# Output products on one TensorE: who makes the low parts, where the conditioning steps and the norm weights stand

## The reference

```python
# conditioning of each layer: six vectors, one per 1024 columns
m = silu(c) @ w_ada + b_ada                      # shift, scale, gate (attention); shift, scale, gate (feed-forward)
# layer 0
new = x + g_a * (concat(oa, ob) @ w_out)         # the output product
h = rmsnorm(new) * (1 + sc_f) + sh_f
new = new + g_f * ((silu(h @ w_gate) * (h @ w_up)) @ w_ffn_out)
# layers 1 and 2
x = layer_norm(ALPHA * x + m[2] * (att @ w_out), ln_g, ln_b)
f = conv_ffn(x * (1 + m[4]) + m[3], w_up, conv_w, conv_b, w_down)
x = layer_norm(ALPHA * x + m[5] * f, ln_g, ln_b)
```

## Time and profile before

| | us |
|---|---|
| median of 3 runs | 2566.37 (2564.48 to 2567.72) |
| profiled execution | 2561.57 |
| its span, first to last instruction | 2559.8 |
| TensorE matmul busy | 2373.7 (93%) |
| VectorE busy | 1601.5 (63%) |
| ScalarE busy | 969.5 (38%) |
| POOL busy | 361.4 (14%) |
| mean granted TensorE clock | 0.971 of full |

### The profile page before, as it was taken

One profiled execution on the slowest core, in us unless ns is written; L12 is line 12 of the kernel. 1 busy time (PEld: TensorE's weight loads), 2 busy tenths in 40 slices (PEclk: granted clock), 3 DMA queues, 4 the chain that ended last, 5 costly groups with the idle time before them and its releaser, 6 DMA issues.

```text
span 2559.8 us, 33225 instructions
## 1 busy us (share of the span) xinstructions
PE 2373.7 (93%) x13210; PEld 1916.1 (75%) x13210; DVE 1601.5 (63%) x2696; ACT 969.5 (38%) x1792; POOL 361.4 (14%) x355
## 2 busy tenths in 40 slices
PE   6987998999998899898989999999988998999996
PEld 3865566888887778566778888888877776788875
DVE  3538676565656742676768775556454986765455
ACT  4325453322212512567242232322432773424232
POOL 0110102100012200000400213223121000101133
PEclk9999999999999999999999999999999998999998
DMA  6221014744534312111322342333112103332321
GB/s 242 93 95 58 25 58 173 250 157 140 181 106 149 108 50 76 50 48 43 140 71 82 99 140 79 112 115 132 46 70 74 34 30 117 134 115 83 107 91 50
DMA packets 79163, 257.59 MB, mean 101 GB/s; under 512 B 5665, under 2 KB 10401, under 8 KB 70561
## 3 DMA queue, kind: packets, MB, share of 16 engines
q1 hardware_dynamic: 65024, 205.01, 23.3%
q0 software_dynamic: 12688, 46.14, 5.2%
q10 hardware_dynamic: 1296, 4.30, 0.4%
HBM read 246.00 MB, written 9.44 MB: 100 GB/s over the span
## 4 chain that ended last, share of the span: by engine, by line
PE 60%; DVE 13%; issue 10%; ACT 7%; POOL 3%; DMA 2%; POOLq 0%; ACTq 0%; DVEq 0%
PE PS L1036 8%; PE PS L1037 8%; PE PS L1038 8%; PE PS L1107 5%; PE PS L1108 4%; PE PS L1109 4%; PE PS L897 3%; PE PS L800 3%; PE PS L797 3%; PE PS L798 3%; PE PS L910 2%; ACT HT L2354 2%; PE PS L941 2%; DVE SM L1752 2%; PE PS L840 1%
## 5 line engine op out<-in xcount | busy, mean ns | idle before, releaser
L1036 PE MATMUL PS<-HH,WH 128*128 128x512 f32 (+1 forms) x1088 | 424.4, 390 | 13.9 <-DVE WL L1926 6.0
L1037 PE MATMUL PS<-HL,WH 128*128 128x512 f32 (+1 forms) x1088 | 420.7, 387 | 0.0
L1038 PE MATMUL PS<-HH,WL 128*128 128x512 f32 (+1 forms) x1088 | 420.4, 386 | 0.0
L2217 ACT ACTIVATE WH<-STG 128x1024 fp32r<-128x1024 f32 (+1 forms) x204 | 198.9, 1022 | 300.0 <-PE PS L1109 237.3
L1926 DVE TENSOR_TENSOR WL<-STG,WH 128x1024 fp32r<-128x1024 f32 (+1 forms) x204 | 239.0, 1212 | 47.1 <-ACT WH L2217 47.1
L1107 PE MATMUL PS<-WH,AH 128*128 128x512 f32 x616 | 244.5, 397 | 14.1 <-DVE WL L1926 5.0
L1036 PEld LDWEIGHTS PS<-HH,WH 128*128 128x128 f32 x1088 | 207.2, 190 | 57.8 <-issue 9.0
L1108 PE MATMUL PS<-WL,AH 128*128 128x512 f32 x616 | 242.8, 394 | 0.0
L1109 PE MATMUL PS<-WH,AL 128*128 128x512 f32 x616 | 242.5, 394 | 0.0
L1037 PEld LDWEIGHTS PS<-HL,WH 128*128 128x128 f32 x1088 | 207.1, 190 | 41.0 <-issue 1.0
L1038 PEld LDWEIGHTS PS<-HH,WL 128*128 128x128 f32 x1088 | 206.8, 190 | 41.3
(11 more groups left out here) (223 smaller groups left out, 4294.6 us busy)
## 6 DMA issues: line engine op xcount, KB each, us to landing
STG<-in_w_up SPq DMA_DIRECT2D x66, 1024.0 KB, 6.2
ADAW<-in_w_ada SPq DMA_DIRECT2D x96, 512.0 KB, 3.7
STG<-in_w_down SPq DMA_DIRECT2D x20, 1024.0 KB, 5.3
ADAW<-in_w_ada POOLq DMA_DIRECT2D x32, 512.0 KB, 4.0
STG<-in_w_ffn_out SPq DMA_DIRECT2D x10, 1024.0 KB, 6.1
STG<-in_ev_w_in SPq DMA_DIRECT2D x8, 1024.0 KB, 5.2
STG<-in_w_in SPq DMA_DIRECT2D x6, 1024.0 KB, 6.6
spill<-X POOLq DMA_DIRECT2D x10, 512.0 KB, 4.7
```

The costliest lines, as they stand in the source:

```text
L1036: e.matmul(out, h_, hh, start=c == 0, stop=False)
L1037: e.matmul(out, h_, hl, start=False, stop=False)
L1038: return e.matmul(out, l_, hh, start=False, stop=c == 7)
```

## The change

The same sums are computed, with these differences in order and place:

- The high parts of the attention's result get a third slot (`out_place`, REG from column 0 in addition to 10240 and 11264). The high and low parts of three tiles are made before the weights' second half is split, and before the conditioning steps. Part 3 follows behind tile 0, part 4 behind tile 1 and part 5 behind tile 3.
- VectorE makes all low parts, in layer 1 too; POOL none.
- In layer 0 VectorE adds the residual instead of POOL.
- In layer 2 the four residual tiles are scaled two before the tiles and one each behind the norms of tiles 0 and 1.
- In layers 1 and 2 the norm of the last but one tile stands behind the transposed tiles' work on VectorE and ScalarE, before `split_up`.
- In layer 0 no conditioning step is taken beside entries that are downs of two units (26 and 27), on SP, VectorE and TensorE.
- `gained` in layer 1: entry 0 none, entry 1 one tile, entry 2 three, entry 3 two.

```diff
+def out_place(i):
+    return (0, 1, 2, 0, 1, 0)[i]
+def out_place_before(i):
+    return {3: 0, 4: 1, 5: 3}[i]
+def out_made(L):
+    n = len(WOUT_TT[L])
+    return [[x for x in range(3, n) if out_place_before(x) == i] for i in range(n)]
...
 def gained(L, pi):
-    return {(1, 0): LAT[:1], (1, 1): LAT[1:3], (1, 2): LAT[3:] + CTX[:1], (1, 3): CTX[1:], (2, 4): LAT[:1], (2, 5): LAT[1:2],
+    return {(1, 1): LAT[:1], (1, 2): LAT[1:], (1, 3): CTX, (2, 4): LAT[:1], (2, 5): LAT[1:2],
             (2, 6): LAT[2:3], (2, 7): LAT[3:]}.get((L, pi), ())
 def ffn_steps(L, pi):
-    return 0 if L == 1 and pi in (2, 3) else 2
+    q = PLAN[L][pi]
+    return 0 if (L == 1 and pi in (2, 3)) or (L == 0 and q[0] == "down" and q[4] == 2) else 2
...
# VectorE, w_out
+        def regain(i):
+            ...                                     # old = old * gain + bias, as before
-        if L != 1:
-            low(0)
-            low(1)
+        for i in range(3):
+            low(i)
         for h in range(2):
             for i in range(2):
                 out_weights_low(L, 1, h, i)
         step(bg, 2 if L else 6)
         if L == 2:
-            ...                                     # all four residual tiles
+            regain(0)
+            regain(1)
         for i, tt in enumerate(WOUT_TT[L]):
             if i == last:
                 turn_mid(L, 0)
-            if L == 0 and i:
+            if i and (L == 0 or i == last):
                 after(WOUT_TT[L][i - 1])
             if i == last:
                 split_up(L, 0)
...
-                if L:
+                if L == 0:
+                    w.wait_ge(*k.dv_yg(("wo", L, tt, n)))
+                    w.wait_ge(*k.old_in[tt](("wo", L)))
+                    old = k.kept(tt)[:, n * 512:(n + 1) * 512]
+                    e.tensor_tensor(old, old, y, ALU.add).then_inc(*k.dv_x.up(("wo", L, tt, n)))
+                else:
...
-            if L != 1 and i + 2 < len(WOUT_TT[L]):
-                low(i + 2)
-            if L:
+            for x in out_made(L)[i]:
+                low(x)
+            if L and i != last - 1:
                 after(tt)
+            if L == 2 and i + 2 <= last:
+                regain(i + 2)
             step(bg, (1, 2, 1, 0)[i] if L == 0 else int(i < 4))
# ScalarE, w_out: high(0) to high(2) ahead, then the same order of high, turn_mid, norm, split_up
# POOL, w_out: low() and the eight additions of layer 0 are gone
```

More of the change, by code:

```diff
@@ L261, in __init__ @@
         self.pl_x = sig("pl_x")
-        self.pl_xl = sig("pl_xl")
         self.pl_gate = sig("pl_gate")
@@ L641, in ffn @@
                 fetch(pi + 1)
-            step(bg, 0 if L == 1 and pi < 4 else 2)
+            step(bg, 0 if L == 1 and pi < 4 else ffn_steps(L, pi))
         step(bg, 100)
@@ L1152, in ffn @@
                             freed[b] = [k.dv_yg((L, g, hh, tt))]
-            step(bg, 2)
+            step(bg, ffn_steps(L, pi))
         step(bg, 100)
@@ L1932, in after @@
             if L == 0:
-                rms(("mid", tt), tt, [k.pl_x(("wo", 0, tt, n)) for n in range(2)], src=k.kept(tt))
+                rms(("mid", tt), tt, [k.dv_x(("wo", 0, tt, n)) for n in range(2)], src=k.kept(tt))
             else:
@@ L1943, in low @@
                 e.tensor_tensor(xl[:, x], k.x(tt)[:, x], xh[:, x].bitcast(F32), ALU.subtract).then_inc(*k.dv_xl.up((L, tt, h)))
+        def regain(i):
+            tt, gain = LAT[i], k.ln_gain("f", 1)
+            old = k.residue(L, i)
+            w.wait_ge(*k.old_in[tt](("wo", L)))
+            w.wait_ge(*k.old_lg_in[0](("f", 1)))
+            e.tensor_tensor(old, old, gain[:, 0:1024], ALU.mult).then_inc(*k.dv_old.up(("mul", i)))
+            w.wait_ge(*k.dv_old(("mul", i)))
+            w.wait_ge(*k.old_lg_in[1](("f", 1)))
+            e.tensor_tensor(old, old, gain[:, 1024:2048], ALU.add).then_inc(*k.dv_old.up(i))
         for s in k.ends(("att", L)):
             w.wait_ge(*s)
-        if L != 1:
-            low(0)
-            low(1)
+        for i in range(3):
+            low(i)
         for h in range(2):
@@ L2472, in norm @@
             if L == 0:
-                o = 1024 * (tt % 2)
-                rms(("mid", tt), tt, k.reg(0, o, o + 1024), [k.pl_x(("wo", 0, tt, n)) for n in range(2)], k.kept(tt))
+                o = 1024
+                rms(("mid", tt), tt, k.reg(0, o, o + 1024), [k.dv_x(("wo", 0, tt, n)) for n in range(2)], k.kept(tt))
             else:
@@ L2480, in high @@
             tt = WOUT_TT[L][i]
-            if i >= 2:
-                w.wait_ge(*k.pe_wout((L, WOUT_TT[L][i - 2])))
+            if i >= 3:
+                w.wait_ge(*k.pe_wout((L, WOUT_TT[L][out_place_before(i)])))
             for h in range(2):
@@ L2488, in w_out @@
             w.wait_ge(*s)
-        high(0)
-        high(1)
+        for i in range(3):
+            high(i)
         for h in range(2):
@@ L2494, in w_out @@
         for i, tt in enumerate(WOUT_TT[L]):
-            if i + 2 < len(WOUT_TT[L]):
-                high(i + 2)
+            for x in out_made(L)[i]:
+                high(x)
             if i == last:
                 turn_mid(L, 0)
-            if L == 0 and i:
+            if i and (L == 0 or i == last):
                 norm(WOUT_TT[L][i - 1])
@@ L2754, in w_out @@
         tts = WOUT_TT[L]
-        def low(i):
-            xh, xl = k.out_parts(L, i)
-            for h in range(2):
-                x = slice(h * 512, h * 512 + 512)
-                w.wait_ge(*k.ac_xh((L, tts[i], h)))
-                e.tensor_tensor(xl[:, x], k.x(tts[i])[:, x], xh[:, x].bitcast(F32),
-                                ALU.subtract).then_inc(*k.pl_xl.up((L, tts[i], h)))
-        if L == 1:
-            low(0)
-            low(1)
         if L == 2:
@@ L2779, in w_out @@
             for i in range(len(tts)):
-                if L == 1 and i + 2 < len(tts):
-                    low(i + 2)
                 step(blocks, int(i < 4))
@@ L2786, in spill @@
             for n in range(2):
[L2787 removed]
+                w.wait_ge(*k.dv_x(("wo", 0, tt, n)))
             e.dma_start(t["spill"][tt], k.kept(tt)).then_inc(*k.spilled[tt].up(0))
         step(blocks, 8)
[L2791 to L2797 removed]
+        for tt in LAT:
             spill(tt)
```

16 lines of the change are left out of this document (4 added, 12 removed).

## The result

| | us |
|---|---|
| median of 4 runs, changed kernel | 2526.3 (2516.9 to 2533.3) |
| median of 4 runs, kernel before, same chip | 2565.4 (2562.8 to 2567.7) |
| ratio, 95% interval | 0.9845 (0.9806 to 0.9885) |
| in another set (run e0 below) | 2534.0 against 2561.8, ratio 0.9888 (0.9873 to 0.9902) |
| profiled execution of the changed kernel | 2533.3, span 2531.5, granted clock 0.971 |

A forecast was written before the change was run, and what follows sets the result against it. TensorE, busy 93% of the span, was taken as the bound, so gains come from its waits and half-clock products. Parts of 8.0, 4.7, 10.0, 10.9 and 1.2 make 34.8, less 3.2 for clock: 2535 us forecast, range 2524 to 2550.

The forecast's parts named there:

- Part 1: Layer 0 feed-forward: without conditioning steps beside two-unit downs, a 5.96 us wait and 2.1 of half clock go; gain 8.0.
- rival B: Moved conditioning steps stall TensorE at their new places by the same 8.0 us, giving 2543; chance 0.06.
- Part 2: Layer 0 output stage: third slot and new order remove a 5.9 us wait for tile 2's low part; gain 4.7.
- Part 3: Layer 1 output stage: third slot, low parts off POOL and deferred norm bring the first up product sooner; gain 10.0.
- Part 4: Layer 2 output stage: earlier low part, spread residual tiles and deferred norm; 12.4 less 1.5 given back, gain 10.9.
- Part 5: Layer 1 feed-forward: later norm weights shrink the 3.3 us wait at entry 3, partly met again later; gain 1.2.
- The clock: New short waits in the changed stages can drop TensorE's clock; two drops charged at 1.6 us each, 3.2.
- Rival A: Output stages: new waits take half of what parts 2 to 4 free (25.6 to 13), giving 2547; chance 0.22.
- Rival C: VectorE becomes the engine that ends every output stage, making the kernel slower, 2582; chance 0.03.
- Rival D: Waits only move to the next product and part 1 alone counts, giving 2558; chance 0.05.

The follow-up runs named there:

- e0: The changed kernel run again without any edit, in another set: median 2534.0 us, ratio 0.9888 to the kernel before.
- e9: The changed kernel with conditioning steps put back beside layer 0's two-unit down products: ratio 0.9921 to the kernel before.
- e2: The changed kernel with the last-but-one tile's norm again ahead of the others' transposing in layers 1 and 2: ratio 0.9928 to the kernel before.
- e3: The changed kernel with layer 1's low parts made by POOL again, three ahead of its loads: ratio 0.9885 to the kernel before.
- e10: The changed kernel with two slots for high parts instead of three, low part of tile i+2 behind tile i: ratio 0.9893 to the kernel before.
- e5: The changed kernel with tile 2's low part late: behind six conditioning steps in layer 0, four residual tiles in layer 2; ratio 0.9897 to the kernel before.
- e4: The changed kernel with the `gained` table (norm weights per entry) as in the kernel before: ratio 0.9902 to the kernel before.
- e11: The changed kernel with layer 0's eight residual additions of the output stage on POOL again: ratio 0.9878 to the kernel before.

## Why the prediction was right, point by point

- **Part 1, 8.0 forecast.** The wait of 5.96 went and came back with the steps (e9), and no wait of TensorE over 0.5 us is new in that stretch, so the moved steps stalled nothing: rival B is out. The stretch lost 7.8 us of idle time, some of it elsewhere, but got 2.3 of half-clock cost at other places; net 5.6. The error is the 2.1 credited for the clock as if no drop would come elsewhere for the one that goes. One cost in these entries was left out of the sum and stayed hidden behind TensorE's work: beside POOL's additions a WL took 4.23 where 2.35 is usual.

```profile
764.09 4.23 DVE L1943 TENSOR_TENSOR WL<-STG,WH 128x1024 fp32r<-128x1024 f32 x2
```

- **Part 2, 4.7 forecast, 2.6 measured,** and between none and 5.3 in the other traces of the same code. The wait of about 2 us before the conditioning columns was named and charged, and measured 1.85. VectorE came to tile 0's product 24.5 us into the stage, as in the sum (24.6). The mis-sized term in this trace is the clock: the sum of this part had none, and behind the wait the transposes and the start of tile 3 ran at half clock, which cost 3.4 where the stage had 1.7 before. TensorE's window there, and the 16 transposes, which take 2.27 in layer 2:

```profile
430.00:434.00 4.00, 4.00 (x19) 0.50 0.46 187
```

```profile
430.14 3.65 PE L1043 MATMUL PS<-CON,X 128*128 128x128 f32 x16
```

In e0 VectorE's chain itself starts late, behind a load, and nothing of the gain is left.
- **Part 3, 10.0 forecast, 9.75 measured.** The transposes in one piece, tile 5 right behind, full clock: each as said. The new wait was 1.36 for a forecast 0.7. By its own terms the sum has tile 5 start at 1277.6, not 1277.2; the trace had it still earlier. Single causes: the norm's place 3.5 (e2), POOL's low parts with the loads behind them 3.8 (e3), the third slot none (e10). The remaining 2.4 needs two of them together or is not accounted for. The Trainium skill (SBUF — State Buffer, Who interferes with whom) says that a VectorE instruction with two SBUF inputs contends with a GpSimd one that reads SBUF. The traces agree: the longest addition took 3.35 us in e3, with POOL's subtractions, and 0.69 in the changed kernel, without.
- **Part 4, 10.9 forecast, 13.1 measured:** 14.3 by the first up product less the 1.2 of new idle time behind it (wait 1.28, forecast 1.5). The last stretch has 2.7 more half-clock cost too, but not behind a wait of this part, and in e0 it is missing. The forecast had 12.4 at the up product; VectorE came to its first tile 16.6 us into the stage, where the sum has 18.6, as the residual load landed earlier. Single causes: the norm's place about 7 (e2), the order with the residual tiles 3.2 (e5), the slot at most 1.1 beside 1.4 of late load (e10), and these overlap.
- **Part 5, 1.2 forecast, about 0 measured.** The forecast had the wait fall under 1.5 and a second one of 2 appear. The first came as 0.89 and 0.82 and the second as 1.25; in e0 as 2.53 and 0.50, so that sign failed there. The sum of 2.96 or 3.03 stands against 3.32 before: the wait was moved and not removed. The later wait for LOW grew from 1.8 to 2.6, in e4 too, where part 5 is undone, so it isn't part 5's.
- **The clock, 3.2 charged.** The half-clock cost rose by 3.2 in all, but that compares with a sum that had already been credited with 2.1 and 1.7, and only the 1.7 more of layer 0 stand at a new wait. Over the traces it lies between 43 and 61 us. The difference between the two sets of medians, 39 and 28 us, goes with the granted clock (0.971 to 0.980 in the first set, 0.970 to 0.973 in the second).
- **Rival A** (new waits eat half): in layer 0 half was eaten, in layers 1 and 2 not. **Rival C:** VectorE stood idle 2.65 and 2.36 us, waiting for the products of tiles 3 and 4 of layer 1, so it doesn't end that stage. **Rival D** (the waits only move) held for part 5, and in layer 0 in e0, and is out for the whole: idle time fell by 27.8 us.

The chance of 0.62 went to a sum whose idle part was right to 4 us (31.0 forecast, 27.8 measured) and whose errors partly cancelled: parts 1, 2 and 5 were 5.7 too high, part 4 2.2 too low, and the 3.2 charged for the clock met 2.7 lost in stretches that no part was about. That the first median, 2526.3, still lies in the range, 2 us over its lower end, is luck of the clock; the second, 2534.0, is the forecast's.

## What to carry to other kernels

Ask of each wait what stands ahead of the awaited instruction on its engine. Moving one norm behind the emptying of a bank was worth more (3.5 and some 7 us of a stage) than moving work from one engine to another (3.8 in e3, none seen in e11), and a stage with 9 us of waits gave nearly all of them back. Sum idle time and half-clock cost apart: over two traces of the changed kernel idle time differed by 2.7 us, 1.8 of it in the stage that follows loads, and by 0.1 or less in the other two output stages; the half-clock cost varied by far more over the traces of this study, and differences under some 0.2% of the whole weren't told apart. Where a wait is filled with work that follows loads, expect a part of it to return as a wait for those loads.

## What the runs showed of the hardware

Whether the same wait costs a clock drop differs from run to run. In two traces of the changed kernel TensorE waits for TMP in layer 2 (2.47 us, until 2150.88; in e0 2.49, until 2157.52). Windows round it, first the changed kernel's first trace, then e0:

```profile
2150.00:2153.00 3.00, 2.12 (x7) 0.84 0.02 5
2153.00:2157.00 4.00, 4.00 (x14) 0.69 0.00 0
2157.00:2162.00 5.00, 5.00 (x24) 1.00 0.84 256
```

```profile
2156.00:2160.00 4.00, 2.48 (x11) 1.00 0.02 4
2160.00:2164.00 4.00, 4.00 (x20) 1.00 0.01 2
```

In the first the clock goes from 2.4 to 1.2 GHz soon after the wait and back (means of 0.84 and 0.69 over the windows, 14 matmuls in 4 us); in the second it stays at 2.4 (20 matmuls). That is 1.6 of the 2.7 us by which the last stretch costs more in the first trace. The rest stands behind another pair, a wait for AL of 3.11 us in both traces, first the changed kernel's first trace, then e0:

```profile
2431.00:2437.00 6.00, 4.61 (x14) 0.72 0.41 131
```

```profile
2435.00:2442.00 7.00, 4.59 (x20) 1.00 0.33 109
```

So the length of a wait alone doesn't tell the drop, and a price for one in a sum is a price for a chance. Over all traces the half-clock cost was 43 to 61 us, with 157 to 186 us idle and no clear relation between the two: the two traces with the most half-clock cost, e2 (60.5) and e4 (59.4), had 167 and 158 us idle, and the kernel before had 186 idle and 47.9.
